# Experts of a decoder trunk in four chunks of 896 columns instead of seven of 512, with the light experts' blocks placed later and their stages in one PSUM bank

## What is computed

```
def _swiglu(h, w_gate, w_up, w_down):
    return (jax.nn.silu(h @ w_gate) * (h @ w_up)) @ w_down

# D_MODEL 1024, D_FF 3584, N_EXPERTS 8, TOP_K 2
logits = xf @ router
top_logits, top_idx = lax.top_k(logits, TOP_K)
gates = softmax(top_logits)
...
yb = _swiglu(x_pad[tok], w_gate[e], w_up[e], w_down[e])     # every expert
out = segment_sum(y * slot_gate, slot_tok)
```

## Time and profile before

| what | value |
|---|---|
| median of 3 runs | 1532.95 us (1532.92 to 1535.02) |
| profiled execution, its own time | 1534.3 us |
| its span from first to last instruction | 1532.5 us |
| TensorE busy | 1459.7 us, 95% |
| VectorE, ScalarE, GpSimd busy | 908.1, 731.3, 316.8 us |
| mean DMA rate over the span | 306 GB/s |

### The profile page before, as it was taken

The page is one execution under the profiler, slowest core; times in us unless marked ns, Lnnn a source line. Parts: engine busy times, 40 slices in busy tenths (PEclk is TensorE's granted clock), DMA queues, the critical chain, the costliest instruction groups (busy, mean ns, idle before and its releaser), DMA issues.

```text
span 1532.5 us, 22560 instructions
## 1 busy us (share of the span) xinstructions
PE 1459.7 (95%) x9592; PEld 1133.1 (74%) x9592; DVE 908.1 (59%) x678; ACT 731.3 (48%) x613; POOL 316.8 (21%) x295
## 2 busy tenths in 40 slices
PE   9999999999999999999999999999999999999995
PEld 8887889999988878788766666666566666666663
DVE  5555566755557857888555555555455554555555
ACT  5444444443345436777444444444444443444443
POOL 5599234400026302980000000000000000000002
PEclk9999999999999999999999999999999999999998
DMA  9645538865531085999999999999999999999993
GB/s 346 185 165 165 191 129 299 287 214 184 183 108 58 31 311 183 376 392 386 380 389 397 397 402 400 394 398 398 399 392 400 400 392 401 387 396 400 395 406 139
DMA packets 187933, 469.61 MB, mean 306 GB/s; under 512 B 7880, under 2 KB 20384, under 8 KB 173488
## 3 DMA queue, kind: packets, MB, share of 16 engines
q1 hardware_dynamic: 183760, 454.57, 79.5%
q0 software_dynamic: 3920, 13.44, 2.7%
q10 hardware_dynamic: 144, 0.07, 0.0%
HBM read 462.02 MB, written 15.21 MB: 311 GB/s over the span
## 4 chain that ended last, share of the span: by engine, by line
PE 67%; DMA 17%; DVE 7%; ACT 5%; issue 2%; POOL 1%; POOLq 0%; SPq 0%; DVEq 0%; ACTq 0%
PE PS L2018 64%; DMA weights_raw<-in_moe_w_down 7%; DMA weights_raw<-in_moe_w_gate 5%; DVE weights_lo L1499 4%; ACT weights_hi L1059 4%; DMA weights_raw<-in_moe_w_up 3%; PE PS L2214 1%; POOL b_padded L879 1%; PE PS L2421 1%; DVE act_rows L1499 0%; DMA row_back<-results_by_slot,pair_index 0%; DMA results_by_slot<-small_expert_rows 0%; ACT c_padded L1059 0%; DVE residual L1499 0%; DVE residual L1900 0%
## 5 line engine op out<-in xcount | busy, mean ns | idle before, releaser
L1499 DVE TENSOR_TENSOR weights_lo<-weights_raw,weights_hi 128x2048 fp32r<-128x2048 f32 (+1 forms) x293 | 677.6, 2315 | 505.9 <-ACT weights_hi L1059 504.8
L1059 ACT ACTIVATE weights_hi<-weights_raw 128x2048 fp32r<-128x2048 f32 (+1 forms) x293 | 559.0, 1909 | 607.7 <-PE PS L2018 201.2
L2018 PE MATMUL PS<-weights_hi,gathered_hi 128*128 128x512 f32 x560 | 226.7, 405 | 31.4 <-DVE weights_lo L1499 28.4
L2018 PE MATMUL PS<-weights_hi,gathered_lo 128*128 128x512 f32 x560 | 222.0, 396 | 0.0
L2018 PE MATMUL PS<-weights_lo,gathered_hi 128*128 128x512 f32 x560 | 222.0, 396 | 0.0
L2018 PE MATMUL PS<-weights_hi,act_transposed_hi 128*128 128x512 f32 x456 | 186.2, 408 | 12.5 <-DVE weights_lo L1499 12.5
L2018 PE MATMUL PS<-x_transposed_hi,weights_hi 128*128 128x256 f32 x640 | 181.1, 283 | 1.2 <-DVE weights_lo L1499 1.0
L2018 PE MATMUL PS<-weights_hi,act_transposed_lo 128*128 128x512 f32 x456 | 180.5, 396 | 0.0
L2018 PE MATMUL PS<-weights_lo,act_transposed_hi 128*128 128x512 f32 x456 | 180.4, 396 | 0.0
L2018 PE MATMUL PS<-x_transposed_lo,weights_hi 128*128 128x256 f32 x640 | 179.6, 281 | 0.0
L2018 PE MATMUL PS<-x_transposed_hi,weights_lo 128*128 128x256 f32 x640 | 179.6, 281 | 0.0
(11 more groups left out here) (328 smaller groups left out, 1466.2 us busy)
## 6 DMA issues: line engine op xcount, KB each, us to landing
weights_raw<-in_moe_w_up SPq DMA_DIRECT2D x111, 1024.0 KB, 11.0
weights_raw<-in_moe_w_down SPq DMA_DIRECT2D x111, 1024.0 KB, 10.1
weights_raw<-in_moe_w_gate SPq DMA_DIRECT2D x110, 1024.0 KB, 10.9
weights_raw<-in_ret_w_in SPq DMA_DIRECT2D x24, 1024.0 KB, 6.8
weights_raw<-in_ffn_w_gate SPq DMA_DIRECT2D x14, 1024.0 KB, 5.1
weights_raw<-in_ffn_w_up SPq DMA_DIRECT2D x14, 1024.0 KB, 5.0
weights_raw<-in_ffn_w_down SPq DMA_DIRECT2D x14, 1024.0 KB, 4.9
weights_raw<-in_ret_w_out SPq DMA_DIRECT2D x8, 1024.0 KB, 4.9
```

The lines of the kernel that those rows point to most:

```text
L1059: return nc.scalar.activation(o, i, ACT.Copy)
L1499: return nc.vector.tensor_tensor(o, a, b, op)
L2018: return nc.tensor.matmul(o, l, r, start=start, stop=stop)
```

## The change

- An expert is done in four chunks of 896 columns. A gate or up unit is 2 k-tiles x 896 columns (1792 floats of each partition, rows of 3.5 KB), in matmuls of 512 and of 384 columns. The seven row tiles of a down chunk lie next to each other in a partition, and go in units of 1, 2, 2 and 2 tiles (4 KB or 8 KB each partition). A stage has 4 units in two blocks, an expert 48 units in 24 blocks.
- PSUM: gate takes banks 0 and 1, up and the turned product banks 2 and 3. An expert's rows are turned at once through banks 0 and 1.
- Light stages share bank 6: gate, then up, then the turned product. ScalarE writes SiLU(gate) to `act_small` and VectorE multiplies there. The turn of the product is 14 matmuls of 64x64 with the identity in place of 2 transposes of 128x128, and stands between the two units of the whole block behind the up stage's second block. Light stages run gate, up, down, chunk by chunk.
- The light blocks start behind whole block 27 (`START = 27`), rank 4's fourth, and end four blocks before the end; they are 72 over 88 whole ones.
- SyncE waits for `experts_known` in place of `shares_ready` ahead of rank 4; GpSimd loads the first rows of slots earlier.

```
+EC = 896
+ESTEPS = FF // EC
+EFT = EC // P
-LAG = 2
+START = 27
...
-    turn, at = divmod(k - LAG, 5)
+    turn, at = divmod(k - START, 5)
...
+def down_tiles(u):
+    return (0,) if u == 0 else (2 * u - 1, 2 * u)
+def unit_width(kind, u):
+    return len(down_tiles(u)) * D if kind == "down" else 2 * EC
...
+            def expert_source(w_gate, w_up, w_down, kind, s, u):
+                if kind == "down":
+                    rows = w_down[s * EC:(s + 1) * EC, :].rearrange("(p k) n -> p k n", p=P)
+                    return rows[:, down_tiles(u)[0]:down_tiles(u)[-1] + 1, :]
+                w = w_gate if kind == "gate" else w_up
+                return w[2 * u * P:(2 * u + 2) * P, s * EC:(s + 1) * EC].rearrange("(k p) n -> p k n", p=P)
...
+            def expert_columns(n, u, bank, e):
+                for k in range(2):
+                    kt = 2 * u + k
+                    for b, c in enumerate((slice(0, 512), slice(512, EC))):
+                        hi, lo = (w[:, k, c] for w in w_parts)
+                        ins = product3(PS[:, bank + b, 0:c.stop - c.start], xg_hi[:, kt, :], xg_lo[:, kt, :], hi, lo,
+                                       kt == 0, kt == KT - 1)
...
+            def turn_small(j):
+                if kind == "up" and part:
+                    pe.wait_ge(mult_small, ESTEPS * LIGHT.index(q) + s + 1)
+                    for ft in range(EFT):
+                        for t in small_tile:
+                            ins = mm(PS[t, 6, ft * SMALL_SLOTS:(ft + 1) * SMALL_SLOTS], act_small[t, ft:HALF_EC:EFT], ident[t, t],
+                                     True, True)
+                    ins.then_inc(turned_small, 1)
...
+                elif kind == "up" and part:
+                    act.wait_ge(turned_small, done + 1)
+                    copy(act_t_small[:, :, :], PS[:, 6, 0:HALF_EC].rearrange("p (f c) -> p f c", f=EFT)).then_inc(act_small_ready, 1)
```

More of the change, by code:

```diff
@@ L88, in block_of, with unit_of @@
     return ranks[k // len(BLOCKS)], k % len(BLOCKS)
+def unit_of(blocks, i):
+    kind, s, part = blocks[i // 2]
+    return kind, s, 2 * part + i % 2
+def down_tiles(u):
+    return (0,) if u == 0 else (2 * u - 1, 2 * u)
+def unit_width(kind, u):
+    return len(down_tiles(u)) * D if kind == "down" else 2 * EC
 def units_in_order():
-    order = [(FIRST, i) for i in range(FFN_UNITS)]
-    for k in range(len(HEAVY) * len(BLOCKS)):
-        for ranks, at in ((HEAVY, k), (LIGHT, small_after(k))):
+    order = []
+    for k in range(len(WHOLE) * len(BLOCKS)):
+        for ranks, at in ((WHOLE, k), (LIGHT, small_after(k))):
             if at is not None:
@@ L1377, in last_y_out, with gather_small @@
                 copy(y_rows[:, 0:512], PS[:, 4, :]).then_inc(y0_copied, 1)
[L1379 to L1383, removed]
+            def gather_small(q):
+                act.wait_ge(gathered, 1 + TURNS.index(q))
+                copy(x_small[:, :, :], PS[:, 6, :].rearrange("p (b c) -> p b c", c=SMALL_SLOTS)).then_inc(x_small_ready, 1)
@@ L1385, in after_small @@
             def after_small(j):
                 q, b = block_of(LIGHT, j)
[L1388 to L1398, removed]
+                kind, s, part = SMALL_BLOCKS[b]
@@ new lines, in expert_block @@
+                    pe.wait_ge(act_lo, count(s0 + s + 1, e, ESTEPS))
+                for i in range(2):
+                    u = 2 * part + i
+                    if i and between:
+                        between()
+                    if kind == "down":
+                        expert_rows(n[i], s, u, e, ends and s == ESTEPS - 1 and u == 3)
+                    else:
+                        expert_columns(n[i], u, 0 if kind == "gate" else 2, e)
+            small_tile = [slice(SMALL_SLOTS * h, SMALL_SLOTS * (h + 1)) for h in range(2)]
@@ L2246, in small_block @@
             def small_block(j):
                 q, b = block_of(LIGHT, j)
-                kind, s = BLOCKS[b]
-                done = STEPS * (q - LIGHT[0]) + s
-                tile = [slice(SMALL_SLOTS * h, SMALL_SLOTS * (h + 1)) for h in range(2)]
-                def landed_unit(half, kt):
-                    n = NUMBER[q, 2 * b + half]
+                kind, s, part = SMALL_BLOCKS[b]
+                done = ESTEPS * LIGHT.index(q) + s
+                if kind == "gate" and part == 0 and s == 0:
+                    pe.wait_ge(x_small_ready, LIGHT.index(q) + 1)
@@ new lines, in small_block @@
+                if kind == "up" and part == 0:
+                    pe.wait_ge(silu_small, done + 1)
+                if kind == "down" and part == 0:
+                    pe.wait_ge(act_small_ready, done + 1)
+                    if s == 0 and q > LIGHT[0]:
+                        pe.wait_ge(y_small_copied, LIGHT.index(q))
+                    if s == ESTEPS - 1 and q < LIGHT[-1]:
+                        turn_small_slots(q + 1)
+                for i in range(2):
+                    u = 2 * part + i
+                    n = NUMBER[q, 2 * b + i]
```

457 lines of the change are left out of this document (210 added, 247 removed).

## The result

The changed kernel takes 1570.82 us (median of 4 runs, 1566.29 to 1576.2), the kernel before in the same runs 1533.99 us (4 runs, 1532.92 to 1536.92). The ratio is 1.0238 with a 95% interval of 1.0195 to 1.0282: the change makes the kernel slower by 2.4%, 37 us, where 12 us less had been predicted. The profiled execution took 1576.2 us, its span is 1574.4 us.

A forecast was written before the change was run, and what follows sets the result against it. Bound by TensorE in the front, then by DMA in the mixed stretch (whole and light blocks). Front +6, mixed -18, end 0 sum to -12: 1521 us, own range 1515 to 1528, wider range 1509 to 1540.

The forecast's parts named there:

- Front: Routed part up to the first light block, set by TensorE: 146.4 us against 140.6, +6.
- Rows of 3.5 KB: Gate and up rows move at 406 GB/s; by DMA the mixed stretch takes 724.7 us, 24 us less.
- Light turn: Turn of the light product on TensorE: 1.6 us each, twelve take 19.4 us against 8.2, +11 us.
- TensorE's need of 720 us: TensorE's work in the mixed stretch: 705 + 1.5 + 11 + 2 = 720 us, against 724.7 of DMA.
- The end: Behind the last light block: four whole blocks and an unchanged chain, 46 us to the end, so 0.
- the overlap: Mixed stretch: DMA's 724.7 us and TensorE's 720, up to 731 with its waits; 731 taken, -18.
- Against a full DMA queue such a wait is partly hidden by the six raw buffers: TensorE's waits behind ScalarE's copy of the turned light product: six of 1.8 us, 11 us, partly hidden.
- The slower rival: Light turn in one bank costs 3.2 us, six waits show, late buffers starve DMA 4 us; 1544 us, chance 0.20.
- The last sentence of the prediction: Signs of a wrong forecast: 3.5 KB rate near 386, turn over 2.6 us, or DMA share well below 1.

The follow-up runs named there:

- experiment 4: Kernel before with light stages in order gate, up, down in one PSUM bank and the turn between the next whole block's two units: 1543.37 us.
- experiments 1 and 2: Changed kernel with ScalarE's copy of the turned light product behind the next split, 1559.22 us; changed kernel with 2 of 14 matmuls in each light turn, 1550.4 us.
- experiments 3 and 8: Changed kernel with nine raw buffers, 1518.86 us; the same with ScalarE's copy of the turned light product behind the next split, 1514.73 us.

## Why the prediction was wrong, point by point

- **Front, +6 us:** right, 147.5 us against 146.4 worked out. TensorE's idle time in it is 3.3 us, where 2.6 was set down.
- **Rows of 3.5 KB, 406 GB/s by the line between 2 and 8 KB:** right. 407 in a stretch of gate and up rows alone, 405 to 408 over the whole window with nine buffers, where the mix of all rows was put at 410.9. The rule of three cycles in the Trainium skill, "DMA: Bandwidth & Descriptors", "Why small descriptors are slow (HBM only)", would give 2% between rows of 2 and of 3.5 KB; the rows say 5.4% (407 against 386), so the measurement decides against it here. (Between rows of 2 and 8 KB the rule comes to 3.5%, where the prediction has 3.4.)
- **Light turn, 1.6 us:** a little small. The 12 turns are one group of 336 instructions, 22.2 us busy, so 1.85 us each and 14 us more than before in place of 11:

```profile
L2038 PE MATMUL PS<-constants,small_act_rows 64*64 64x64 f32 x336 | 22.2, 280 | 5.9 <-DVE small_act_rows L1531 5.7
```

- **TensorE's need of 720 us:** right, in part by luck. It is busy for 731.8 us, of which 12.0 us are its lower clock, below. The turns were 3 us too small in the sum, but the 705 us that it starts from hold 2.8 us of work ahead of the mixed stretch; in the 749 us themselves TensorE was busy for 702.4:

```profile
737.50:1486.50 749.00, 702.37 (x3717) 481.52 (x3716) 394.71 (x238) 338.13 (x263) 5.98 (x11) 1.00 1.04 396
```

- **The end, 0:** right.
- **The step that failed** is the overlap: "Two limits so near to each other add a little to both; I take 731", together with the clause "Against a full DMA queue such a wait is partly hidden by the six raw buffers". Both take the cover of six buffers as what it was. The diff's own numbers, six buffers and 48 units an expert in place of 42, make it 5.5 MB for 6.3 MB, and neither sum nor range had that term. Of the 53 us by which the mixed stretch was longer than forecast, some 42 are idle time of TensorE (52.6 us for 11) and some 12 its lower clock. One buffer more, which makes up for the bytes, gives back 33 us. With a ring that is deep enough the sum holds: nine buffers give 1518.86 us, where 1521 was predicted, in a mixed stretch of 728.4 us with TensorE idle for 10.7, where 731 and 11 were. In that state the change is worth 9.7 us against the kernel before with nine buffers as well (1528.6).
- **The slower rival** (1544) had the right mechanism in its last clause, "the raw buffers of light units are freed later, which starves DMA", at about 4 us. One more buffer gives back 33 us, so it was mis-sized by a factor of eight or so, since it was tied to the turn and not to the ring's bytes. The two conditions that it named were not what decided: a turn takes 1.85 us and not 3.2, and the one bank with its held copy costs the kernel before 8 us (experiment 4).
- **The last sentence of the prediction** said that DMA's share falling well below 1 "because buffers come free late" would make it wrong. That is the direction that the row shows, 0.98 for 1.04, though the step is small.

What stays open: how the 37 us divide between the smaller ring and the light order cannot be read off as a sum. One buffer gives back 33, the copy 12, the turns 20, more than there are together, because each counts almost in full in a loop that is short, and the last two hardly at all when it is not. Units of 1 MB in a ring of six, with the rest of the change, were not tried.

## What to carry to other kernels

When a change alters the size of a unit, count the ring in bytes and not in buffers: rate times time to land is what has to be in flight (here some 4 MB for 396 to 399 GB/s), and what is landed and in use (some 2 to 2.5 MB with five to seven buffers, 3.6 MB with nine) comes on top. A landing time that falls together with the DMA rate, while TensorE and DMA both have idle time, is the sign that the ring is too small; the chain looks the same with full DMA engines. Test with one buffer less in the kernel before: that costs one run and separates the ring from all else. And do not take the saving of an experiment that leaves work out as proof of a bound before the ring is deep enough.

## What the runs showed of the hardware

In the changed kernel TensorE's clock goes to its lower level (1.2 for 2.4 GHz) for a few us at a time, as here, after TensorE had been idle for 1 of the 4 us in the row before. The matmuls of 512 columns that follow start 0.42 us apart, then 0.24 again:

```profile
1110.00:1114.00 4.00, 3.05 (x28) 2.34 (x29) 2.75 (x3) 0.00 (x0) 0.00 (x0) 1.00 0.94 375
1114.00:1118.00 4.00, 4.00 (x21) 3.21 (x20) 1.23 (x1) 3.29 (x3) 0.00 (x0) 0.61 0.81 340
```

```profile
1116.20 0.63 PE L2038 MATMUL PS<-weights_lo,act_transposed_hi 128*128 128x512 f32 x1
1116.62 0.63 PE L2038 MATMUL PS<-weights_hi,act_transposed_lo 128*128 128x512 f32 x1
...
1118.33 0.40 PE L2038 MATMUL PS<-weights_hi,act_transposed_hi 128*128 128x512 f32 x1
1118.57 0.40 PE L2038 MATMUL PS<-weights_lo,act_transposed_hi 128*128 128x512 f32 x1
```

Cut into stretches of 25 us from 800 to 1400, nine of 24 show a mean clock under 1.00, five of them 0.93; one minus the clock, times 25 us, adds up to 12 us. In steps of 2 us over the window of 744 to 1470 there are seven such episodes in the changed kernel (12.0 us in all) and twelve in the one with five buffers (20.5 us), but three and two in experiments 1 and 2 (5.1 and 3.4 us), three in experiment 4, and none or one in the kernel before and in all kernels with seven or nine buffers (at most 1.7 us). So the ring that is too short costs twice here, first the wait and then the clock behind it. It also goes with the wider spread: the four runs of the changed kernel, 1566.29 to 1576.2 us, have mean clocks of 0.992 to 0.986 in the same order.

What brings the clock down stays open. Over the window TensorE is idle for 46 us in the kernel before and for 51 us in the changed one, so the share of idle time does not tell them apart. Of the seven episodes three start right behind a light turn that had waited some 0.95 us for VectorE's product, and four behind a wait of 1.8 to 3.3 us for a split. The light turn is not the cause by itself: the kernels of experiments 3 and 8 have all twelve turns and one episode each, the one with five buffers has none of these turns and twelve episodes. The Trainium skill, "TensorE: Matmul & The Clock Gate", "HAM oscillation — how this bites in real kernels", describes a clock that falls in a kernel whose matmuls wait for DMA again and again. The trace agrees in part: ahead of three of the seven episodes the split itself had waited for a unit to land, but ahead of the one shown here (0.61) TensorE's last wait was for VectorE. The prediction had no term for it.
